# Giving the 20th place in the order of experts to the overfull one, so that its second block finds the weights in the ring

## What is computed

```python
def hier_moe(h, p):
    t = h.reshape(-1, d)                                  # 384 x 1024
    lg = t @ p['w_rg'] + p['b_rg']                        # 4 groups, one is picked
    le = (t @ p['w_re'] + p['b_re']).reshape(-1, 4, 8)    # 8 experts in a group, two are picked
    ...                                                   # gate: 384 x 32, two entries of a row are not zero
    h1 = jnp.einsum('td,edf->tef', t, p['w1'])            # 32 experts, 1024 x 256
    h3 = jnp.einsum('td,edf->tef', t, p['w3'])
    hh = jax.nn.silu(h1) * h3 * gate[:, :, None]
    return jnp.einsum('tef,efd->td', hh, p['w2'])         # 256 x 1024
```

## Time and profile before

| | us |
|---|---|
| median of 3 runs | 1073.49 (1071.4 to 1083.82) |
| the profiled execution | 1074.82 |
| its span, first to last instruction of the core | 1073.0 |
| busy: TensorE matmul, VectorE, ScalarE, GpSimd | 911.1, 388.0, 238.9, 120.6 |
| mean granted TensorE clock, share of full | 0.929 |
| moved by DMA | 324.97 MB, mean 303 GB/s |

### The profile page before, as it was taken

One profiled execution on the slowest core, in us unless ns is written; L12 is line 12 of the kernel. 1 busy time (PEld: TensorE's weight loads), 2 busy tenths in 40 slices (PEclk: granted clock), 3 DMA queues, 4 the chain that ended last, 5 costly groups with the idle time before them and its releaser, 6 DMA issues.

```text
span 1073.0 us, 14096 instructions
## 1 busy us (share of the span) xinstructions
PE 911.1 (85%) x5389; PEld 521.3 (49%) x5389; DVE 388.0 (36%) x1099; ACT 238.9 (22%) x598; POOL 120.6 (11%) x131
## 2 busy tenths in 40 slices
PE   5899788986999885998589988987779998859980
PEld 1345346546555543554266553554465555535540
DVE  1112466344622221221264565662455221202214
ACT  3110143111111110111344453441111111101111
POOL 1000000100122111121100000001001222111210
PEclk9999899996999997999889998998879999989996
DMA  9979798365989999899850056017599899999984
GB/s 379 398 276 407 308 417 332 118 230 190 363 305 397 415 416 416 360 414 391 314 200 6 1 219 252 11 37 263 206 402 367 329 407 418 415 390 414 415 333 183
DMA packets 69835, 324.97 MB, mean 303 GB/s; under 512 B 12566, under 2 KB 13590, under 8 KB 46600
## 3 DMA queue, kind: packets, MB, share of 16 engines
q1 hardware_dynamic: 54304, 292.14, 68.5%
q0 software_dynamic: 13328, 25.02, 6.9%
q10 hardware_dynamic: 2144, 7.02, 1.7%
HBM read 318.97 MB, written 26.49 MB: 322 GB/s over the span
## 4 chain that ended last, share of the span: by engine, by line
PE 63%; DMA 21%; DVE 10%; ACT 3%; issue 2%; SPq 1%; POOL 0%; POOLq 0%; DVEq 0%; ACTq 0%
PE psum L773 16%; DMA ring<-in_l_w 13%; PE psum L786 8%; PE psum L969 7%; PE psum L723 4%; DMA ring<-in_l_w_ada 3%; PE psum L753 2%; PE psum L1084 2%; PE psum L1075 2%; PE psum L1025 2%; PE psum L614 2%; PE psum L1116 2%; PE psum L736 1%; PE psum L744 1%; DMA scale_shift<-gate_rows_hbm 1%
## 5 line engine op out<-in xcount | busy, mean ns | idle before, releaser
L773 PE MATMUL psum<-ring,scratch 128*64 128x256 f32 x1920 | 225.4, 388 | 26.3 <-DMA ring<-in_l_w 24.6
L773 PEld LDWEIGHTS psum<-ring,scratch 128*64 128x64 f32 x1920 | 143.1, 139 | 93.7 <-issue 35.9
L1933 DVE TENSOR_TENSOR scratch<-scratch,psum 64x256 f32<-64x256 f32 x64 | 27.2, 425 | 315.2 <-ACT scratch L1333 315.1
L786 PE MATMUL psum<-ring,scratch 128*64 128x512 f32 x496 | 119.9, 604 | 2.6 <-ACT scratch L1337 1.9
L2378 POOL DMA_INDIRECT expert_rows<-scratch,slot_rows x64 | 63.7, 995 | 333.9 <-ACT scratch L1347 322.2
L1333 ACT ACTIVATE scratch<-psum 64x256 f32<-64x256 f32 x64 | 24.1, 376 | 258.5 <-PE psum L773 258.5
L969 PE MATMUL psum<-ring,scratch 128*128 128x512 f32 x192 | 74.6, 548 | 1.3 <-DVE scratch L2054 1.3
L1347 ACT COPY scratch<-psum 128x512 f32<-128x512 f32 x64 | 37.5, 586 | 146.7 <-PE psum L786 146.7
L614 PE MATMUL psum<-ring,scT 128*32 128x512 f32 x320 | 42.6, 655 | 15.8 <-DMA ring<-in_l_w_ada 14.7
L969 PEld LDWEIGHTS psum<-ring,scratch 128*128 128x128 f32 x192 | 36.8, 194 | 37.4 <-issue 36.3
L786 PEld LDWEIGHTS psum<-ring,scratch 128*64 128x64 f32 x496 | 31.0, 136 | 44.9 <-issue 39.9
(11 more groups left out here) (319 smaller groups left out, 1136.8 us busy)
## 6 DMA issues: line engine op xcount, KB each, us to landing
ring<-in_l_w SPq DMA_DIRECT2D x186, 1024.0 KB, 16.5
ring<-in_l_w_ada SPq DMA_DIRECT2D x48, 1024.0 KB, 12.9
ring<-in_l_w_o SPq DMA_DIRECT2D x8, 1024.0 KB, 12.6
ring<-in_l_w_in SPq DMA_DIRECT2D x4, 1024.0 KB, 25.6
gate_rows<-gate_rows_hbm POOLq DMA_DIRECT2D x8, 512.0 KB, 10.0
scale_shift<-gate_rows_hbm POOLq DMA_DIRECT2D x8, 512.0 KB, 9.7
scratch<-expert_rows SPq DMA_DIRECT2D x8, 512.0 KB, 5.3
ring<-in_l_w_in SPq DMA_DIRECT2D x4, 768.0 KB, 11.6
```

The lines of the kernel that those rows point to most:

```text
L773: last = nc.tensor.matmul(ps[64 * n:64 * n + 64, 2 + par, 0:DE], mine[:, k, :], part(w, k * DE, DE), start=k == 0, stop=k == KD - 1)
L786: last = nc.tensor.matmul(ps[64 * n:64 * n + 64, 5 + par, :], hhT[:, par, k, :], part(w2, k * D + n * 512, 512), start=k == 0, stop=k == 1)
```

## The change

Routing, on VectorE, now also picks an expert: among those in places 8 to 31 that have over 64 rows, the first one in number (a table of candidates `C_CAND`; `C_HOME` stands for expert 25 where there is none). `twice` is its one-hot row. One block is subtracted from its number of overflow blocks (`nover`), and the numbers of its further blocks move down by one. `route_swap` then exchanges its columns with those of expert 25 in the tables that the one-hots are built from, and writes the exchanged order to `expert_order`. SyncE reads the expert number of places 8 and up from that table before each of their loads, and waits for `route_ready` before place 8.

Block 0 of the overflow is now always run, without `If`, and takes its weights from the ring group of place 19. Its load is gone. Its one-hot block, row numbers and token fetch are moved ahead into the steps of places 18 and 19, on VectorE, TensorE and GpSimd. Further blocks, if any, load their weights as before, from b = 1. Place 22, which takes the slots of place 19, now waits for `ov_passed`, as place 23 does. `load_pairs` also waits for the write of block 0. The constants are 64 columns wider.

```diff
+HOME = (HEAD - 1) // 2 + (HEAD - 1) % 2 * PAIRS
+FIXED = 8
...
+    c[:, C_CAND:C_CAND + NE] = np.where(np.arange(NE) % PAIRS * 2 >= FIXED, NE - np.arange(NE), 0)
+    c[:, C_HOME + HOME] = 0.5
...
             def taken(l, q, n):
-                if q == OVER_GROUP:
+                if q in (group(HEAD - 1), OVER_GROUP):
                     sp.wait_ge(S["ov_passed"], l + 1)
...
+            def in_turn(l, column):
+                at = slice(column, column + 1) if isinstance(column, int) else bass.ds(column, 1)
+                return sp.value_load(order[0:1, l, at], min_val=0, max_val=NE - 1)
...
                 for e in range(five + 1, five + 5):
+                    if e == FIXED:
+                        sp.wait_ge(S["route_ready"], l + 1)
+                    mine = block_of(e) if e < FIXED else in_turn(l, block_of(e))
                     for n in range(3):
                         taken(l, group(e) - 4, n)
-                        load_expert(l, block_of(e), group(e) % 4, n).then_inc(arrives(group(e) % 4, n), 16)
+                        load_expert(l, mine, group(e) % 4, n).then_inc(arrives(group(e) % 4, n), 16)
...
-                with sp.If(count > 0):
-                    one(0)
-                sp.end_ifs()
...
                     step(e, *place(e), pair=e // 2)
+                    if e == HEAD - 1:
+                        pe.wait_ge(S[f"ov_dve_steps{l}"], 1)
+                        overflow_tokens().then_inc(S[f"ov_pe_steps{l}"], 1)
                     down_step(e - 1, *place(e - 1))
...
+            def over_matrix(l, b, n):
+                g = group(HEAD - 1) if isinstance(b, int) else OVER_GROUP
+                return ring[:, (S_MOE[l] + 3 * (g % 4) + n) % RING, :]
...
 (route_blocks)
+                link(V.scalar_tensor_tensor(out=twice, in0=cnt, scalar=float(SLOTS), in1=con[:, C_CAND:C_CAND + NE],
+                                            op0=ALU.is_gt, op1=ALU.mult))
+                link(V.tensor_tensor(twice, twice, con[:, C_HOME:C_HOME + NE], ALU.add))
+                link(V.tensor_reduce(taken_from, twice, AX, ALU.max))
+                link(V.tensor_scalar(twice, twice, taken_from, None, ALU.is_equal))
+                link(V.scalar_tensor_tensor(out=first_row, in0=cnt, scalar=float(SLOTS), in1=twice, op0=ALU.is_gt, op1=ALU.mult))
+                link(V.tensor_tensor(nover, nover, first_row, ALU.subtract))
...
 (route_tokens)
-                link(V.scalar_tensor_tensor(out=first_row, in0=ofs, scalar=-1.0, in1=pri, op0=ALU.add, op1=ALU.add))
+                link(V.tensor_tensor(first_row, ofs, pri, ALU.add))
+                V.tensor_tensor(cnt, twice, ofs, ALU.mult)
+                link(V.tensor_tensor(first_row, first_row, twice, ALU.subtract))
                 link(V.tensor_tensor(blk, blk, over(first_row, 1, [P, NT, NE]), ALU.mult))
+                link(V.scalar_tensor_tensor(out=key, in0=jumps, scalar=1.0, in1=over(cnt, 1, [P, NT, NE]),
+                                            op0=ALU.is_equal, op1=ALU.mult))
+                link(V.tensor_tensor(blk, blk, key, ALU.subtract))
...
+            def route_swap(l):
+                for table in (slotm[:, :, 0:NE], row_numbers):
+                    link(V.tensor_tensor(le, table, over(twice, 1, [P, NT, NE]), ALU.mult))
+                    link(V.tensor_reduce(top[0], le, AX, ALU.add))
+                    link(V.tensor_tensor(top[1].unsqueeze(2), table[:, :, HOME:HOME + 1], top[0].unsqueeze(2), ALU.subtract))
+                    link(V.tensor_tensor(le, over(twice, 1, [P, NT, NE]), over(top[1], 2, [P, NT, NE]), ALU.mult))
+                    link(V.tensor_tensor(table, table, le, ALU.add))
+                    link(V.tensor_copy(table[:, :, HOME:HOME + 1], top[0].unsqueeze(2)))
+                ids, named = iota[0:1, 0:NE], cnt[0:1, :]
+                link(V.tensor_tensor(named, ids, twice[0:1, :], ALU.mult))
+                link(V.tensor_reduce(taken_from[0:1, :], named, AX, ALU.add))
+                link(V.scalar_tensor_tensor(out=named, in0=ids, scalar=-float(HOME), in1=twice[0:1, :], op0=ALU.add, op1=ALU.mult))
+                link(V.tensor_tensor(named, ids, named, ALU.subtract))
+                link(V.tensor_copy(order[0:1, l, :], named))
+                link(V.tensor_copy(order[0:1, l, HOME:HOME + 1], taken_from[0:1, :]))
...
 (experts, VectorE)
                 product(1, 1)
                 ahead(1, 0, 1)
+                route_swap(l)
                 route_overflow(l)
...
+                    if e == HEAD - 2:
+                        one_hot_block(0, S[f"ov_dve_steps{l}"])
+                    if e == HEAD - 1:
+                        overflow_rows(l, 0)
...
 (GpSimd, places)
                         fetch_tokens(l, e // 2 + 2)
+                    if e == HEAD - 2:
+                        fetch_overflow(l, 0)
                     put_rows(l, e)
```

More of the change, by code:

```diff
@@ L211, in trunk @@
         ovi = sb("overflow_blocks", N_LAYERS, 16, dt=i32)
+        order = sb("expert_order", N_LAYERS, NE, dt=i32)
         gates = sb("gates", NT, 2)
@@ L518, in one @@
                     sp.sem_inc(S["ov_turns_sp"], 1)
-                with sp.If(count > 0):
-                    one(0)
-                sp.end_ifs()
                 with sp.If(count > 1):
-                    with sp.Fori(1, OVER) as b:
+                    with sp.Fori(1, OVER + 1) as b:
                         with sp.If(b < count):
@@ L537, in load_pairs @@
             def load_pairs(l):
+                sp.wait_ge(S[f"ov_out{l}"], 16)
                 for buf in range(2):
@@ L874, in experts @@
                 down_step(NE - 1, *place(NE - 1))
-            def over_matrix(l, n):
-                return ring[:, (S_MOE[l] + 3 * (OVER_GROUP % 4) + n) % RING, :]
+            def over_matrix(l, b, n):
+                g = group(HEAD - 1) if isinstance(b, int) else OVER_GROUP
+                return ring[:, (S_MOE[l] + 3 * (g % 4) + n) % RING, :]
             def overflow(l):
                 pe.wait_ge(S["route_ready"], l + 1)
-                count = pe.value_load(ovi[0:1, l, 15:16], min_val=0, max_val=OVER)
+                count = pe.value_load(ovi[0:1, l, 15:16], min_val=1, max_val=OVER + 1)
+                pe.wait_ge(S[f"ov_dve_steps{l}"], 2)
                 def one(b):
-                    pe.wait_ge(S[f"ov_dve_steps{l}"], b * 4 + 1)
-                    overflow_tokens().then_inc(S[f"ov_pe_steps{l}"], 1)
+                    if not isinstance(b, int):
+                        pe.wait_ge(S[f"ov_dve_steps{l}"], b * 4 + 1)
+                        overflow_tokens().then_inc(S[f"ov_pe_steps{l}"], 1)
                     pe.wait_ge(S[f"ov_x{l}"], b * 16 + 16)
@@ L895, in one @@
                     pe.wait_ge(S[f"ov_act_steps{l}"], b * 3 + 2)
[L896 to L900, removed]
+                    down(0, over_matrix(l, b, 2)).then_inc(S[f"ov_pe_steps{l}"], 1)
+                one(0)
                 with pe.If(count > 1):
-                    with pe.Fori(1, OVER) as b:
+                    with pe.Fori(1, OVER + 1) as b:
                         with pe.If(b < count):
@@ L1383, in one @@
                     nc.scalar.copy(y_over, ps[:, 5, :]).then_inc(S[f"ov_act_steps{l}"], 1)
-                with act.If(count > 0):
-                    one(0)
-                act.end_ifs()
+                one(0)
                 with act.If(count > 1):
-                    with act.Fori(1, OVER) as b:
+                    with act.Fori(1, OVER + 1) as b:
                         with act.If(b < count):
@@ L2002, in one @@
                     dve.sem_inc(S[f"ov_free{l}"], 1)
-                with dve.If(count > 0):
-                    one(0)
-                dve.end_ifs()
+                one(0)
                 with dve.If(count > 1):
-                    with dve.Fori(1, OVER) as b:
+                    with dve.Fori(1, OVER + 1) as b:
                         with dve.If(b < count):
@@ L2395, in one @@
                         .then_inc(S[f"ov_out{l}"], 16)
-                    pool.wait_ge(S[f"ov_out{l}"], b * 16 + 16)
-                    pool.sem_inc(S["ov_turns_pool"], 1)
-                with pool.If(count > 0):
-                    one(0)
-                pool.end_ifs()
+                    if not isinstance(b, int):
+                        pool.wait_ge(S[f"ov_out{l}"], b * 16 + 16)
+                        pool.sem_inc(S["ov_turns_pool"], 1)
+                one(0)
                 with pool.If(count > 1):
-                    with pool.Fori(1, OVER) as b:
+                    with pool.Fori(1, OVER + 1) as b:
                         with pool.If(b < count):
```

55 lines of the change are left out of this document (33 added, 22 removed).

## The result

| | before | after |
|---|---|---|
| median, us | 1074.15 (4 runs, 1071.4 to 1083.82) | 1091.16 (4 runs, 1087.98 to 1096.62) |
| ratio | 1 | 1.0143 [1.0107, 1.0178] |
| profiled execution, its span | 1074.82, 1073.0 | 1092.64, 1090.7 |

The change makes the kernel 1.4% slower. By the ratio the time is 1073.49 x 1.0143 = 1088.8 us, near the upper end of the range of 1070 to 1091; the bare median of 1091.16 lies at its very edge. Between the two profiled spans lie 17.7 us, where the prediction has 9.1 and the ratio gives 15.3.

The account below looks back on a forecast made before the run. The weights' stream was taken to bound the kernel. Routing's 2 x 5.9 = 11.8 us less the overflow's 2.7 gave +9.1 on 1073.5, so 1082.6 us; range 1070 to 1091, most likely 1078 to 1088 (0.5).

Parts of the forecast that it names:

- What bounds the kernel: Experts of a layer: the weights' stream is the bound; TensorE's 9.0 us stall before the overflow is largely hidden.
- Routing: VectorE, places 0 to 2: 28 instructions, 6.5 us, delay TensorE 4.2 us; with 1.7 us for the clock, 5.9 per layer.
- one drop: TensorE behind the 2.9 us idle stretch before place 2: clock falls to 1.2 GHz, costing 1.7 us, bounds 0 and 3.4.
- Rival 2: Routing costs more: two clock drops per layer or delay reaching place 3, 2 x 3 us more, 1089; chance 0.17.
- The anchor: Full ring at 310.4 to 319.4 us: TensorE delay before that point moves the whole stream and the layer's end.
- SyncE: 24 order reads per layer and the `route_ready` wait before place 8: taken at nothing; reads without cover 7 us.
- The overflow: 7.6 us of stream saved per layer, spent as idle DMA from 421.6 to 427.4 us; gains 0.5 and 2.2 us.
- taken back: Token landing to first weight issue, 12.5 us before: 1.2 us less through a shorter idle time, bounds 0 and 3.
- The sum: Whole kernel: 11.8 us from routing less 2.7 from the overflow, +9.1 us, giving 1082.6 us.
- One side sum of the prediction: By the VectorE page's table, 28 instructions cost 3.7 us, TensorE's delay 1.4 without clock drop, total near +0.4.
- Rivals 1 and 3: Rival 1 has its own line; rival 3: swap misses the block, exposing a full one, over 20 us per layer, 1115; 0.04.
- Rival 1: Place 22 issued by 421.6 us, stream keeps about 10 us per layer, 1065, chance 0.07; milder case about 1076, 0.22.

Follow-up runs that it names:

- the fetch a place sooner: Kernel with spread routing and ring slots dealt anew, plus overflow one-hot, row numbers and token fetch one place earlier: 1060.02 us, ratio 0.9863 to the kernel before.
- the spare transposes: Changed kernel plus 14 unused transposes on TensorE before the transposes of places 0 and 2: 1089.66 us, ratio 1.014 to the kernel before.
- routing alone: Kernel before plus the 28 added VectorE routing instructions, results unused, order and overflow as before: 1090.48 us against 1074.13, ratio 1.0131.
- the slots dealt anew: Changed kernel, place 20 taking the three empty slots, so only place 23 waits for `ov_passed`; one ring group skipped before place 28: 1078.55 us, ratio 1.0032.
- the kernel with both repairs: Changed kernel with routing spread over places 0 to 3 and ring slots dealt anew: 1064.43 us, ratio 0.9895 to the kernel before.

## Why the prediction was right, and where its sizes were off

**What bounds the kernel: right.** The stream of weights is the bound and TensorE's stall of 9.0 us was mostly hidden in it. Where the stall falls to 1.2 us (the fetch a place sooner), the overflow's stage gets 5.4 and 6.0 us shorter, and what follows it gets longer by all but 0.4 and 0.7 us of that. The one wait of place 22, which stops no engine but SyncE where it stands, loses 1.1%.

**Routing: the mechanism right, the size 5.9 against a measured 6.9 us per layer.** The 28 instructions take 6.9 us where 6.5 were forecast. This is read with the spare transposes, where nothing else delays VectorE: the product of place 2 starts 22.81 us behind the first up instead of 16.53, and uses up 0.65 us in which VectorE was idle before. `route_swap` takes 4.38 us of it, against 4.3. VectorE's delay of TensorE without any slow up is therefore 4.66 us against the 4.2 of the sum: so much is left both with the spare transposes (30.53 - 25.87) and in the layer whose clock stayed up by itself (30.23 - 25.57). The wait before place 2 was forecast at 2.9 us; it was 3.11 where the up of place 1 ran at full clock and 2.04 where it did not, since TensorE was late itself. The rest of the miss is the clock. The step took one drop, behind an idle stretch of 2.9 us, and set the one at place 0 aside. Both came in both layers, behind waits of 1.84 to 2.15 us. If the later one costs its full 1.7 us, the earlier has 6.9 - 4.66 - 1.7 = 0.5 us left, since TensorE would have waited for VectorE at place 2 in any case. Rival 2, two drops, was therefore right in what happens in the changed kernel, and wrong in its price of 3 us more per layer: both drops and VectorE's delay are 1.0 us more together. That both came was in part chance, as the layers with one drop or none show.

On what sets the clock, the page "TensorE: Matmul & The Clock Gate" of the Trainium skill, section "Why this matters for your kernels", advises to keep long idle gaps out between bursts of matmuls. The gap from which it warns is longer than the 2.15 us that came before a slow up here, so by it neither drop would have come and routing would have cost 4.7 us a layer. The trace has both outcomes.

**The anchor: right.** Places 4 to 10 take 40.39 us everywhere. With routing alone the delay of 6.9 and 7.6 us made before them is one of 6.1 and 7.6 at place 31, and the kernel's ratio is 1.0131.

**SyncE: right,** 1.0007 [0.9986, 1.0029] with all its reads and the wait. In the changed kernel a read takes 0.27 us (ns, min/median/max):

```profile
L458 SPq TENSOR_LOAD <-expert_order x48: 262/273/468, 290.6 to 1030.7; - x48
```

**The overflow: the hole is there, the gain in front of it isn't.** The DMA share falls to 0.28 and 0.01 in the 12 us from 423 us on. Its timing is as forecast: the last transfer ahead of the hole is issued at 416.3 us and lands 12.6 us later, at 428.9, which is the forecast 421.6 plus the 7.2 us by which place 10 starts later here. The share falls before that, from 421 us on, while the last transfers are still on their way. The forecast counted landings and left that out.

The term that was mis-sized is the time from the landing of the tokens to the first weight issue, and in it the 1.2 us "taken back" for the clock. The changed kernel needs 435.02 - 422.65 = 12.4 us in layer 0 and 974.33 - 961.96 = 12.4 in layer 1, where 11.3 and 10.8 were forecast and the kernel before needed 12.5 and 12.0. Nothing was taken back: the up of the block still took 5.16 us in both layers, at a granted clock of 0.53 and 0.50 around its start, behind stalls of 3.8 and 4.0 us, as behind the one of 9.0. These are 1.1 and 1.6 us of the 4.0 by which the forecast gain of 0.5 + 2.2 us and the measured loss of 0.5 + 0.8 differ. The other 1.3 us are not traced to a step.

The single wait of place 22 shows how much a hole eats, and the slots dealt anew show the other side: with the same bytes and the hole mostly closed, the stage behind the overflow is 7.5 and 7.8 us shorter. The forecast had given the hole about this length (5.8 us dry and 2.3 until the stream runs again).

**The sum.** Against 9.1 us: routing 2 x 1.0 more, the overflow 2.7 + 1.3 = 4.0 more, the slow last up of layer 1 another 1.7, which no step had. That gives 16.8; the other 0.9 us lie outside the experts and weren't followed up. The forecast put the kernel at 1082.6, most likely in 1078 to 1088, and it is above both. What happened was rival 2's drop together with no gain at the overflow, which as a sum was not drawn up. All misses go the same way, so that the time still lies in the range is owed to the range's width as much as to the sum. One side sum of the prediction is off by itself: by the table of the page on VectorE it should come to 2 x 1.4 - 2.7 = +0.1 instead of +9.1 us, and not to "+0.4 instead of +9.4".

**Rivals 1 and 3: did not occur.** Rival 1's condition, place 22 issued before the stream is dry, isn't met by the change. Its price of about 10 us per layer was too high: the kernel with both repairs, with three places on the way, runs a layer 8.1 and 5.3 us faster, and the one that fetches a place sooner, with hardly a hole, 8.9 and 6.6. Of each, 0.6 and 0.3 us are gained in places 0 to 4, before the overflow.

## What to carry to other kernels

Before work is moved ahead, see which consumer stands behind it in its engine's queue: 28 short instructions cost 1.3% ahead of the products of places 0 and 2, and nothing when all of routing was dealt out between four. Where a stream is the bound, a stall of the compute engine may be hidden, as most of the 9 us was here, and a new hold on ring slots is not; count how many transfers are still allowed while the hold lasts, and compare their time with the hold. Here the saving in bytes counted only once the hole was mostly closed, so close the hole first and only then shorten the stall.

## What the runs showed of the hardware

- How long TensorE had waited did not decide its clock. In layer 1 of the changed kernel a wait of 1.84 us stood before an up of 5.36 us (granted clock 0.50, or 1.2 GHz, from 815.3 to 817 us in it). With the slots dealt anew the same wait, and even one of 3.11 us, stood before ups of 3.67 us (1.00, 2.4 GHz), in code that is the same there. With routing alone a wait of 3.11 us stood before an up of 6.31 (0.50 from 830.7 to 834 us). In the weight-bound stretch of layer 1 of the changed kernel the up behind 2.18 us was slow and one behind 2.60 us, two places sooner, was not. What tells them apart stays open. For a forecast, such a drop, of 1.7 us or with the longest up 2.6, is a chance and not a term. Lines of the changed kernel's timeline:

```profile
812.95 0.44 PE L793 MATMUL psum<-constants,scratch 128*128 128x128 f32 x2 [1.84 <-DVE scratch L1981]
813.32 5.36 PE L787 MATMUL psum<-ring,scratch 128*64 128x256 f32 x32
1040.51 3.67 PE L787 MATMUL psum<-ring,scratch 128*64 128x256 f32 x32 [2.60 <-DMA ring<-in_l_w]
```

- With 14 transposes (1.73 us) in each early wait all four ups of that profile took 3.67 us; in layer 0 they stood behind the 0.56 and 1.43 us that were left, at a granted clock of 1.00 (2.4 GHz). Since the clock stayed up once without them too, this run alone doesn't show that they did it.
- A short VectorE instruction costs by its count: 28 of them take 6.9 us, for arithmetic over 1 to 96 elements a partition. The page "VectorE: DVE Perf Modes" of the Trainium skill, section "The TRN2 errata — SBUF-src ops pay a fixed extra latency per instruction", has a measured formula from which an estimated 0.26 us follows at 96 elements; the trace agrees (0.26 at 281.84).
